# Moving the low-weight ring and one FFN buffer by 64 bytes, with unused products behind the last group

## The reference

```
for l in range(DEPTH):                                   # DEPTH = 2
    p = rmsnorm(x, norm_mix[l]) @ w_in[l]                # 2048 x 4608
    y_b = diff_attention(q, k, v, ...)                   # 8 heads of 128, block-causal chunk mask
    y_a = multiscale_pool(a_in, pool_w[l], pool_scale[l])
    y_c = conformer_conv(c_in, ...)                      # causal depthwise conv of 31 taps, LayerNorm
    x = x + concat(y_b, y_a, y_c) @ w_out[l]             # 2048 x 2048
    gu = rmsnorm(x, norm_ffn[l]) @ w_ffn_in[l]           # 2048 x 11008
    g = causal_dwconv(gu[..., :D_FF], ffn_conv_w[l], ffn_conv_b[l])
    x = x + (silu(g) * gu[..., D_FF:]) @ w_ffn_out[l]    # 5504 x 2048
return rmsnorm(x, final_norm)
```

## Time and profile before

| | before |
|---|---|
| median of three runs | 2080.04 us |
| profiled execution: span from the first to the last instruction | 2078.2 us |
| TensorE busy | 2064.8 us, 99% of the span |
| TensorE weight loads busy | 1792.4 us, 86% |
| VectorE busy | 1415.6 us, 68% |
| ScalarE busy | 1081.7 us, 52% |
| GpSimd busy | 23.5 us, 1% |
| HBM traffic | 188 GB/s over the span |

### The profile page before, as it was taken

One profiled execution on the slowest core, in us unless ns is written; L12 is line 12 of the kernel. 1 busy time (PEld: TensorE's weight loads), 2 busy tenths in 40 slices (PEclk: granted clock), 3 DMA queues, 4 the chain that ended last, 5 costly groups with the idle time before them and its releaser, 6 DMA issues.

```text
span 2078.2 us, 32569 instructions
## 1 busy us (share of the span) xinstructions
PE 2064.8 (99%) x11564; PEld 1792.4 (86%) x11564; DVE 1415.6 (68%) x2009; ACT 1081.7 (52%) x1509; POOL 23.5 (1%) x20
## 2 busy tenths in 40 slices
PE   9999999999999999999999999999999999999998
PEld 8888888888888888888888888888888888888886
DVE  7998777676666666555489978676666676654454
ACT  6556655555555554433374566455555555544444
POOL 0001100000000000000000011000000000000000
PEclk9999999999999999999999999999999999999999
DMA  8554455655555555555666544655555655565664
GB/s 290 179 183 159 139 183 182 204 190 192 192 182 192 191 192 193 193 197 179 207 209 196 177 145 145 198 190 192 191 184 182 202 189 195 183 212 193 194 199 163
DMA packets 108944, 392.66 MB, mean 189 GB/s; under 512 B 12225, under 2 KB 12737, under 8 KB 108481
## 3 DMA queue, kind: packets, MB, share of 16 engines
q1 hardware_dynamic: 106992, 386.45, 56.6%
q10 hardware_dynamic: 1872, 5.13, 0.8%
HBM read 389.43 MB, written 2.10 MB: 188 GB/s over the span
## 4 chain that ended last, share of the span: by engine, by line
PE 99%; DMA 0%; DVE 0%; ACT 0%; ACTq 0%; issue 0%; DVEq 0%
PE bank L1179 53%; PE bank L1182 27%; PE bank L1458 4%; PE bank L1457 4%; PE bank L1456 4%; PE bank L1266 2%; PE bank L1255 1%; PE bank L1256 1%; PE bank L1257 1%; DMA x<-xT 0%; PE bank L1319 0%; PE bank L1431 0%; PE bank L1342 0%; DVE xt L1131 0%; DVE wlo L716 0%; ACT whi L364 0%
## 5 line engine op out<-in xcount | busy, mean ns | idle before, releaser
L736 DVE TENSOR_TENSOR wlo<-raw,whi 128x1024 fp32r<-128x1024 f32 x728 | 885.8, 1222 | 609.5 <-ACT whi L406 608.6
L1179 PE MATMUL bank<-xg,whi 128*128 128x512 f32 x3648 | 1135.6, 393 | 1.9 <-DVE wlo L716 1.9
L406 ACT ACTIVATE whi<-raw 128x1024 fp32r<-128x1024 f32 x728 | 764.2, 1057 | 693.3 <-PE bank L1182 558.0
L1182 PEld LDWEIGHTS bank<-xg,wlo 128*128 128x128 f32 x3648 | 685.0, 188 | 151.3
L1182 PE MATMUL bank<-xg,wlo 128*128 128x256 f32 x3648 | 720.1, 279 | 0.0
L1179 PEld LDWEIGHTS bank<-xg,whi 128*128 128x128 f32 x3648 | 552.9, 188 | 6.3 <-issue 3.3
L1179 PE MATMUL bank<-hidden,whi 128*128 128x512 f32 x688 | 213.5, 392 | 0.0
L1179 PE MATMUL bank<-mix,whi 128*128 128x512 f32 x512 | 160.7, 395 | 0.0
L1182 PEld LDWEIGHTS bank<-hidden,wlo 128*128 128x128 f32 x688 | 129.2, 188 | 28.5
L1182 PE MATMUL bank<-hidden,wlo 128*128 128x256 f32 x688 | 135.8, 279 | 0.0
L1456 PE MATMUL bank<-whi,hidden 128*128 128x512 f32 x344 | 134.6, 391 | 0.0
(11 more groups left out here) (150 smaller groups left out, 1140.8 us busy)
## 6 DMA issues: line engine op xcount, KB each, us to landing
raw<-wstream SPq DMA_DIRECT2D x729, 512.0 KB, 3.4
pw_sb<-pww ACTq DMA_DIRECT2D x2, 1024.0 KB, 7.3
outT<-xt SPq DMA_DIRECT2D x8, 256.0 KB, 2.9
x<-xT SPq DMA_DIRECT2D x2, 512.0 KB, 10.3
gains<-gain_rows ACTq DMA_DIRECT2D x1, 1024.0 KB, 6.3
raw<-wstream SPq DMA_DIRECT2D x2, 256.0 KB, 4.5
x<-xT ACTq DMA_DIRECT2D x2, 256.0 KB, 5.4
x<-xT SPq DMA_DIRECT2D x2, 256.0 KB, 7.3
```

The source lines that it names most:

```text
L406: nc.scalar.activation(whi[:, s, :], raw[:, s, :], ACT.Copy).then_inc(hi_ready, 1)
L736: nc.vector.tensor_tensor(wlo[:, s, :], raw[:, s, :], whi[:, s, :], ALU.subtract).then_inc(lo_ready, 1)
L1179: nc.tensor.matmul(ps[bank][:], whi[:, s, blk * P:blk * P + P], mov, start=first, stop=False)
L1182: return nc.tensor.matmul(ps[bank][:, 0:S], wlo[:, s, blk * P:blk * P + P], mov[:, 0:S], start=False, stop=last)
```

## The change

It has three parts. A tile `offset4` of 16 elements is put ahead of `wlo`, so `wlo` and all that follows up to `y` begins 64 bytes further on; `offset2` is made 16 elements smaller, so what lies behind it stays. `offset3` is now closed together with the mixers' tiles, so `mix` and the other mixers' tiles stay and `hidden0` begins 64 bytes sooner, where `hidden1` begins. Behind the last group TensorE issues products whose results nobody reads: eight settings of the places of the high and the low weights (offsets in elements inside `hidden1`), six pairs of blocks each, with two products of 512 and two of 256 columns for a pair, into banks 0 to 3.

```diff
         whi = sb("whi", [P, RING, PIECE], f32r)
+        sb("offset4", [P, 16])
         wlo = sb("wlo", [P, RING, PIECE], f32r)
...
-        sb("offset2", [P, 240])
+        sb("offset2", [P, 224])
         until_last_ffn = ExitStack()
-        sb("offset3", [P, 16], f32, until_last_ffn)
         with ExitStack() as mixers:
+            sb("offset3", [P, 16], f32, mixers)
             mix = sb("mix", [P, KC, 2 * S], f32r, mixers)
...
+            flat = hidden1[:].rearrange("p k c -> p (k c)")
+            moving, weights = flat[:, 0:2 * S], flat[:, 4 * S:]
+            probes = [(0, 0, True), (16, 0, True), (0, 16, True), (16, 16, True), (0, 0, False), (12, 12, True), (20, 20, True),
+                      (16, 256 + 16, True)]
+            pe.wait_ge(evacuated, (LAYERS - 1) * TILES + TD + 8 + CREDIT)
+            for hi, lo, paired in probes:
+                for pair in range(6):
+                    blks = (2 * (pair % 2), 2 * (pair % 2) + 1)
+                    order = [("h", b) for b in blks] + [("l", b) for b in blks]
+                    if not paired:
+                        order = [(w, b) for b in blks for w in "hl"]
+                    for w, b in order:
+                        if w == "h":
+                            nc.tensor.matmul(ps[b][:], weights[:, hi + b * P:hi + b * P + P], moving, start=True, stop=False)
+                        else:
+                            nc.tensor.matmul(ps[b][:, 0:S], weights[:, lo + b * P:lo + b * P + P], moving[:, 0:S],
+                                             start=False, stop=True)
```

## The result

The changed kernel takes 2131.89 us (median of 4 runs, 2131.77 to 2132.71) against 2080.05 us for the kernel before (median of 4): ratio 1.0249, 95% interval 1.0235 to 1.0264. That is 51.8 us more. The forecast was 24.5 us more (2104.5 us), so it was right in sign and less than half of the measured change; the measured time lies above its range of 2084 to 2125 us.

The account below looks back on a forecast made before the run. TensorE's pace of products was taken as the bound. Span 2078.2 + 23.0 + 0 + 1.5 = 2102.7 us, plus 1.84 us of median above span, gave 2104.5 us; range 2084 to 2125 us.

Parts of the forecast that it names:

- What bounds the kernel: Whole kernel: TensorE, busy 99% of the span, sets the time; VectorE, ScalarE and the weight stream do not.
- Part 1: Behind the last group: 48 added quads at 690 ns take 33.1 us, partly covered by the tail; +23.0 us.
- Part 2: Group form, 2424 quads: two of four loads change relation to the moving operand; taken as 0, bounds -32 and +32 us.
- low weights alike are dearer: Rival for group form: +3 to +13 ns a quad, 2112 to 2136 us; chance 0.24.
- Part 3: Token form: D of layer 1 +2.3 us, values -0.8 us, together +1.5 us; bounds 0 and +6.8 us.
- Part 4: Tiles from con to y, shifted by 64 bytes: work beside TensorE with idle time as cover, costed at nothing.
- Places do nothing: Rival for operand places: they have no effect, only the added products cost; 2103.1 us; chance 0.12.
- Cheaper: Rival for group form: low weights alike gain; full contrast 2071.8 us, chance 0.08; smaller gain 2083 to 2097 us, 0.14.

Follow-up runs that it names:

- e1: The changed kernel without the added products behind the last group; 2108.41 us, ratio 1.0134 to the kernel before.
- e3: Kernel before with only the low ring (wlo) moved 64 bytes further on, hidden0 left in place, no added products; 2108.95 us, ratio 1.0136.
- e4: Kernel before with only hidden0 moved, 64 bytes sooner; 2082.64 us, ratio 1.0012.
- e5: Kernel before with only hidden1 moved, half a step beside whi and wlo; 2086.74 us, ratio 1.0031.
- e7: Kernel before with only xg moved, onto a whole step; 2090.24 us, ratio 1.0045.
- e8: Kernel before with every place flipped: xg, mix, hidden0 on a whole step, whi, wlo, hidden1 half a step beside; 2086.44 us, ratio 1.0031.
- e10: Kernel before with xg, mix, hidden0 and wlo on a whole step, whi and hidden1 half a step beside; 2107.60 us, ratio 1.0133.
- the fastest pair: Kernel before with whi moved 192 bytes and wlo 304 bytes further on, hidden1 moved with whi; 2107.20 us, ratio 1.0135.
- the grid: Kernel before plus unused products at all 256 pairs of high and low weight places, 0 to 240 bytes in 16-byte steps; one run, 3504.78 us.

## Why the prediction was wrong, by its own steps

**What bounds the kernel.** Right. TensorE's pace was all that mattered, and no other engine's busy time moved by more than 1.7 us.

**Part 1, the products behind the last group.** Right: +23.0 us taken, 23.8 measured in the two spans and 23.9 with the products alone. Of the small rest 0.5 us is that all eight settings ran slower than 690 ns, at 693 to 713; the 48 quads took 33.6 us instead of 33.1. That the setting in another order "has the same products" was no ground for the same price: it ran 11.5 ns a quad slower than the same places in the usual order.

**Part 2, low weights in group form.** This step failed. "I take 0, and keep -32 and +32" stood where about +10 ns a quad were measured, in D of layer 0 as well: the real work ahead of D of layer 1 came 23.0 us later. That the relation of places sets part of the loss was right, and the rival "low weights alike are dearer" with its 3 to 13 ns holds the value; it had a chance of 0.24. The error was in the reasoning that chose the middle. It carried the loss for each product from D of layer 1 (13.4 ns, all alike) over to the quad's changed products, as if a load's loss hung on its own relation alone. The runs show that it does not: both alike costs 697 ns, one alike 700, so the loss of a quad is no sum of two terms. "Alike" and "apart" were too coarse as well: for the low weights of D of layer 0, "apart" before and after, the distance went from -64 to +64 bytes, and 16-byte steps and distances within 256 bytes turned out to count. The range was made by chances over these cases, and was cut at 2125 us although the dearer case alone had been worked out to 2136.

**Part 3, token form.** Right in sign, wrong in size: +2.3 us for D of layer 1 against 5.1 measured. The price of 6.6 ns was near; the count was wrong. 344 products were priced, and all 1032 lose some 5 ns. The bound of +6.8 us, "if a change of relation upsets all three products", was the true case. For the values a gain of 0.8 us was taken; the 384 products lost 0.6 ns each in the real stages (233.4 to 234.0), 0.2 us in all.

**Part 4, the other tiles.** Right: 2079.89 us with them alone moved.

**The rivals.** "Places do nothing" falls: eight kernels in which only places moved (e1, e3 to e5, e7, e8, e10 and the fastest pair) took 2.5 to 29 us more. "Cheaper" falls. With the first falls what the prediction made of the two independent read ports of the Trainium skill, page "TensorE: Matmul & The Clock Gate", section "Step-by-step: what each phase is for", namely that places would change nothing. The added products have nothing of ScalarE's and VectorE's writes into the rings and show the same paces as the real stages, so those writes are not needed for the effect. Of the independent ports the runs say only that the pace hangs on the distance between what the two streams read; what inside the chip makes them meet was not measured.

## What to carry to other kernels

Where TensorE is the bound and weights are loaded under every product, the places of the operands in SBUF belong to the tuning, here up to 1.4% of the time for 64 bytes. Don't carry a loss from one order of products to another: at the same places it was 697.5 and 709 ns a quad. Put a map of the settings behind the kernel as unused products, which costs one run, run it a second time with the settings in another sequence, and then check the candidate in the real stages, for the same places can hold a slower pace behind a break in the stream.

## What the runs showed of the hardware that was not expected

- The mean time of a steady quad mostly came out in steps of about 3.3 ns, 16 columns at 2.4 GHz being 6.7 ns: 686.7, 690, 693.3, 696.7, 700, 703.3, 706.7, 713.3. The single products vary (112 to 128 ns for 256 columns in the grid) in a pattern that repeats.
- The pattern mostly settles within one to three quads of a new setting, and distances that differ by 128 bytes in one operand are not the same: +64, 0 ran at 713.5 ns and +64, +128 at 700.
- One pair of places held two steady paces, 686.7 and 703 ns, for tens and hundreds of microseconds each, and in B of layer 1 took one or the other in two kernels whose programs are the same up to the last group.
- Seven of 40 pairs of distances had another pace in another map, by up to 13.3 ns (700.0 and 713.3 at -64, -32).
